# A kernel for one decoder step: 32 of 384 dense tokens take their first expert layer from fetched rows

## The chip, the cores and the metric

The kernel runs on one core of a Trainium2 chip. The metric is the device time of one execution in microseconds (us). The profile names the engines PE (TensorE, matrix products; PEld is its weight load), DVE (VectorE), ACT (ScalarE), POOL (GpSimd) and SP (SyncE, which here only issues DMAs). All data is float32; a product is formed from rounded "hi" parts and "lo" remainders in three matrix products.

## What is computed

One decoder layer on 512 prompt tokens and 32 sample tokens: attention, an output projection, and then the expert layer (PEER) that this text is about. The reference of the expert layer, cut:

```python
q = (xt @ w_query).reshape(PEER_BLOCK, PEER_HEADS, D_QUERY)      # 8 heads
s1 = einsum("thc,nc->thn", q[..., :half], k1)                    # 128 keys each
s2 = einsum("thc,nc->thn", q[..., half:], k2)
v1, i1 = top_k(s1, 16);  v2, i2 = top_k(s2, 16)
cand = v1[..., :, None] + v2[..., None, :]                       # 256 sums
top, pos = top_k(cand, 16)                                       # 16 of them
eidx = (i1 * 128 + i2) at pos                                    # 16 experts per head
g = softmax(top)
hid = einsum("thkd,td->thk", u_tab[eidx], xt)                    # first expert layer
a = g * gelu(hid)
out = einsum("thk,thkd->td", a, v_tab[eidx])                     # second expert layer
```

Each token has 8 heads of 16 chosen experts, 128 in all, out of 16384. A row of `u_tab` or `v_tab` is 1024 numbers, 4 KB.

## The kernel before, in words

The 544 tokens are tiles of 128 (the last has the 32 samples). Tokens 0 to 127 and the samples are **fetched**: their 160 sets of expert rows (each 128 rows of 4 KB, 512 KB) are gathered by indirect DMAs of POOL, and DVE forms a dot product with each (`multiply`, L1508; "dot" below). Tokens 128 to 511, 384 of them, are **dense**: for each of the 128 tiles of 128 experts PE multiplies all experts with all 384 tokens (`hidden_product`, L1426, 24 matmuls of 384 columns, output `hp`), ACT applies the gelu and a DMA stores the result; a gate matrix, built by small matmuls from one-hot rows, later says which values count.

A tile of `u_experts` (`uw`) has to be split first: ACT rounds it (`uhi`, L1420) and then POOL (L1424) or DVE (L2050) subtracts to get `ulo`. Tile m can't be split before PE is done with tile m - 2, and PE can't begin tile m before `ulo` is there. SP issues the load of tile m once tile m - 4 has been split.

After the attention the order on every engine is written out by hand, in stages:

- **Route.** `route_on_tensor` takes 8 heads in turn: two query products (48 matmuls of 272 columns), two sets of key scores, and 4 dense tiles per head (tiles 0 to 31). ACT copies the scores to `sc`, for which it needs DVE to have read the head before (`qs["read"]`). `route_on_vector` does the selection for a head in 18 linked steps (`LINKS`; each link waits for the one before), and then copies top values and indices (L1795 to L1797). POOL splits tiles and query weights.
- **QX.** 16 more dense tiles (32 to 47). When DVE has ended head 7 it prepares the tables: `first`, a subtraction, `eidx` (L1806), `sample_idx` (L1808), which count in `table_prep`; then SP spreads the sample indices over the partitions, and the softmax follows. Three transposes of `I1`, `I2` and `GG` come behind tiles 45, 46 and 47 on PE (`MIX` is 13); the first two need `table_prep` 2, the third 3.
- **Turns.** Six turns of 12 tiles (48 to 119), each with 16 groups of one-hots (DVE and ACT build them, PE multiplies them, ACT evacuates), 12 splits and 20 or 25 dots on DVE. Before the first turn DVE splits tile 49, builds two groups and does 5 dots (`FIRST_DOTS`).
- **GX.** Tiles 120 to 127 with the last 15 dots.
- **Values.** The second expert layer on PE, about 2,300 matmuls of 512 columns, until the end.

Dots go through nine buffers (`LOOK`): five of `gathered` and four of `vw`. POOL requests row set n + 9 when dot n is done.

## Time and profile before

| | us |
|---|---|
| median of 3 runs | 1698.84 (1697.75 to 1703.23) |
| the profiled execution | 1703.0 |
| its span, first to last instruction | 1701.4 |
| PE busy | 1622.1 (95%) |
| DVE busy | 1353.9 (80%) |
| ACT busy | 777.5 (46%) |
| POOL busy | 613.5 (36%) |
| three line groups of `hp` matmuls (1024 each) | 354.0, 344.8, 343.5 |

The three `hp` groups overlap one another, since matmuls are pipelined: their busy times can't be added, and what a matmul costs is the distance between two starts. The shares are means over stages with different limits, so the stages have to be read one by one.

### The profile page before, as it was taken

Reading aid. Unit: us, or ns where it says so; the run is one execution under the profiler, and the core shown is the slowest. Engines: PE = TensorE matmul, PEld = TensorE weight load, DVE = VectorE, ACT = ScalarE, POOL = GpSimd, SP = SyncE. Lnnn points to the kernel's source line nnn. Section 1 sums busy time; section 2 is a strip of 40 time slices with the busy share of each in tenths; the row PEclk is TensorE's granted clock in tenths of the full one; section 3 lists DMA queues with packets and bytes.
Section 4 is the critical chain, followed back from the end, with each engine's and each line's share of the span. In section 5 each row is a group of like instructions: output and inputs, shape, how many; then the busy total and the mean of one; then the engine's idle time right before and its main releaser. Section 6 shows DMA issues by size and latency. Waiting matters only on the chain.

```text
span 1701.4 us, 27754 instructions
## 1 busy us (share of the span) xinstructions
PE 1622.1 (95%) x9666; PEld 1460.0 (86%) x9666; DVE 1353.9 (80%) x3162; ACT 777.5 (46%) x1273; POOL 613.5 (36%) x538
## 2 busy tenths in 40 slices
PE   5999988798999999989999999999999999999997
PEld 4999744497999999989999999997888888888886
DVE  4324585353799999979999999987999999999996
ACT  4222373233434433367777767753333333333334
POOL 0000380054444444654334334432343333433320
PEclk9999997997999999999999999999999999999999
DMA  3342562722343333499999999999999999999991
GB/s 119 106 164 92 167 190 91 264 89 77 114 148 109 122 114 109 156 364 375 384 372 393 387 367 393 400 405 388 404 403 399 404 404 399 405 403 399 402 366 53
DMA packets 158621, 463.54 MB, mean 272 GB/s; under 512 B 18224, under 2 KB 64432, under 8 KB 154546
## 3 DMA queue, kind: packets, MB, share of 16 engines
q1 hardware_dynamic: 98930, 248.59, 39.7%
q0 software_dynamic: 50944, 178.96, 27.6%
q10 hardware_dynamic: 8640, 34.61, 5.1%
q8 instruction: 62, 1.02, 0.2%
q14 instruction: 45, 0.37, 0.1%
HBM read 406.12 MB, written 57.63 MB: 273 GB/s over the span
## 4 chain that ended last, share of the span: by engine, by line
PE 60%; DVE 13%; POOL 3%; DMA 2%; issue 1%; ACT 1%; another core or an unknown queue 0%; SPq 0%; ACTq 0%; POOLq 0%
PE va L230 10%; PE va L232 10%; PE va L231 10%; PE hp L230 6%; PE hp L231 6%; PE hp L232 6%; DVE gathered L1511 3%; DVE og L2039 3%; DVE ulo L2050 3%; PE ggp L1979 2%; DVE vw L1511 2%; PE qzp L230 2%; PE qzp L232 2%; PE qzp L231 2%; PE qsp L1680 1%
## 5 line engine op out<-in xcount | busy, mean ns | idle before, releaser
L230 PE MATMUL hp<-mid_hi,uhi 128*128 128x384 f32 x1024 | 354.0, 346 | 9.9 <-DVE ulo L2050 3.6
L231 PE MATMUL hp<-mid_lo,uhi 128*128 128x384 f32 x1024 | 344.8, 337 | 0.0
L232 PE MATMUL hp<-mid_hi,ulo 128*128 128x384 f32 x1024 | 343.5, 335 | 0.0
L230 PE MATMUL va<-vhi,ahi 128*128 128x512 f32 x768 | 299.8, 390 | 2.8 <-DVE hid L1511 2.1
L232 PE MATMUL va<-vhi,alo 128*128 128x512 f32 x768 | 299.5, 390 | 0.0
L231 PE MATMUL va<-vlo,ahi 128*128 128x512 f32 x768 | 299.3, 390 | 0.0
L1909 POOL DMA_INDIRECT gathered<-in_v_experts,eidx x160 | 175.6, 1098 | 310.3 <-DVE acc L2359 221.5
L230 PEld LDWEIGHTS hp<-mid_hi,uhi 128*128 128x128 f32 x1024 | 192.9, 188 | 15.0 <-DVE ulo L2050 5.8
L232 PEld LDWEIGHTS hp<-mid_hi,ulo 128*128 128x128 f32 x1024 | 193.0, 188 | 0.0
L231 PEld LDWEIGHTS hp<-mid_lo,uhi 128*128 128x128 f32 x1024 | 192.8, 188 | 0.0
L1420 ACT ACTIVATE uhi<-uw 128x1024 fp32r<-128x1024 f32 x126 | 132.8, 1054 | 116.1 <-PE hp L232 114.6
L1424 POOL TENSOR_TENSOR ulo<-uw,uhi 128x1024 fp32r<-128x1024 f32 x47 | 120.0, 2552 | 151.9 <-ACT uhi L1420 151.8
L230 PEld LDWEIGHTS va<-vhi,ahi 128*128 128x128 f32 x768 | 144.5, 188 | 34.3 <-DVE hid L1511 2.6
L232 PEld LDWEIGHTS va<-vhi,alo 128*128 128x128 f32 x768 | 144.5, 188 | 30.3
L231 PEld LDWEIGHTS va<-vlo,ahi 128*128 128x128 f32 x768 | 144.6, 188 | 30.0
L2359 DVE SCALAR_TENSOR_TENSOR acc<-gathered,coef,acc 128x1024 f32<-128x1024 f32 x128 | 164.2, 1283 | 4.2 <-DMA gathered<-in_v_experts,eidx 1.7
L1490 POOL DMA_INDIRECT gathered<-in_u_rows,eidx x96 | 104.7, 1090 | 165.2 <-DVE hid L1511 151.2
L1925 ACT ACTIVATE vhi<-vw 128x1024 fp32r<-128x1024 f32 x68 | 72.1, 1060 | 135.3 <-PE va L232 130.0
L2146 ACT ACTIVATE gst<-ggp 128x512 f32<-128x512 f32 x96 | 108.2, 1134 | 53.8 <-PE ggp L1979 40.1
L2039 DVE TENSOR_SCALAR og<-iota,chunkT 128x128 f32<-128x128 f32 x384 | 124.5, 367 | 0.0
L1925 ACT ACTIVATE vhi<-more_v 128x1024 fp32r<-128x1024 f32 x60 | 63.6, 1060 | 120.6 <-PE va L232 113.6
L1511 DVE CUSTOM_DVE_ANT_0 gathered<-gathered,x2p 128x1024 f32<-128x1024 f32 x96 | 113.5, 1212 | 5.0 <-DMA gathered<-in_u_rows,eidx 5.0
(328 smaller groups left out, 3448.6 us busy)
## 6 DMA issues: line engine op xcount, KB each, us to landing
uw<-in_u_experts SPq DMA_DIRECT2D x128, 512.0 KB
vw<-in_v_experts SPq DMA_DIRECT2D x68, 512.0 KB
more_v<-in_v_experts SPq DMA_DIRECT2D x60, 512.0 KB
gate_matrix<-gst ACTq DMA_DIRECT2D x12, 2048.0 KB
hidden_values<-gelu_out SPq DMA_DIRECT2D x72, 192.0 KB
hd_mid<-hidden_values SPq DMA_DIRECT2D x8, 1536.0 KB
gt_mid<-gate_matrix SPq DMA_DIRECT2D x8, 1536.0 KB
hd_freed<-hidden_values SPq DMA_DIRECT2D x7, 1536.0 KB
```

Of the source, the lines that this page charges most:

```text
L230: nc.tensor.matmul(out, a_hi, b_hi, start=first, stop=False)
L231: nc.tensor.matmul(out, a_hi, b_lo, start=False, stop=False)
L232: return nc.tensor.matmul(out, a_lo, b_hi, start=False, stop=last)
L1420: nc.scalar.activation(uhi[:, i], uw[:, r], ACT.Copy).then_inc(u_hi, 1)
L1424: nc.gpsimd.tensor_tensor(ulo[:, i], uw[:, r], uhi[:, i].bitcast(F32), ALU.subtract).then_inc(u_lo, 1)
L1490: nc.gpsimd.indirect_dma_start(buffers[to], None, u_table, bass.IndirectOffsetOnAxis(ap=eidx[:, row, b:b + 1], axis=0)).then_inc(gathered[ ...
L1511: nc.vector.tensor_tensor_reduce(out=buffers[to], in0=buffers[to], in1=x2p[:, b // SG], scale=1.0, scalar=0.0, op0=ALU.mult, op1=ALU.add, ...
L1909: nc.gpsimd.indirect_dma_start(gb[:, b], None, v_table, bass.IndirectOffsetOnAxis(ap=eidx[:, r, b:b + 1], axis=0)).then_inc(row_landed[b], 16)
L1925: nc.scalar.activation(vhi[:, m % GT], source, ACT.Copy).then_inc(xs["vhi"], 1)
L2039: last = nc.vector.tensor_scalar(og[:, i % RING, k], iota[:], col(0), col(2), ALU.is_equal, ALU.mult)
L2146: nc.scalar.activation(gst[:, u, :, 4 * r:4 * r + 4].rearrange("p i t -> p t i"), gp[i % 2][:], ACT.Copy).then_inc(gs["ev"], 1)
L2359: nc.vector.scalar_tensor_tensor(acc0[:], gb[:, c], coef[:, r, c:c + 1], acc0[:], ALU.mult, ALU.add).then_inc(xs["s0"], 1)
```

## The change

The last 32 of the 384 dense tokens (tokens 480 to 511, partitions 96 to 127 of token tile 3) take their first expert layer from fetched rows. Their 32 x 128 rows are 32 sets of 128 rows: 4 sets per head (`OWN_SLOTS`), each with 4 groups of 32 partitions. In parts:

1. Every `hp` product is 352 columns wide (`DENSE`) and not 384. The gelu is as wide; the last 32 columns of `gelu_out` are set to 1, once, by POOL.
2. Behind each head's selection DVE writes the 16 expert numbers of these tokens to `own_stage`, and SP spreads them with 4 small DMAs to `own_index` (`own_spread`).
3. POOL requests the 4 sets of head j - 2 in turn j, each behind a split (`own_fetch`); of heads 6 and 7 in QX.
4. DVE forms their 4 dots (`own_dot`) in head j behind links 10, 12, 14 and 16; the dots of heads 6 and 7 stand behind the tables. The tokens' own rows are read from PSUM (`x2own`).
5. ACT applies the gelu to them, SP brings them back with 4 DMAs (`own_act`), and DVE multiplies them into `GG` ahead of `table_prep` 3.
6. The splits of tiles 42 and 43 go from POOL to DVE (`LENT` is 10), behind the first own dots of head 6.
7. Of the 160 other dots 15 come before the turns (`FIRST_DOTS` 15, three of them ahead of `table_prep` 3, nine ahead of tile 49's split), 130 in the turns (`TURN_DOTS`) and 15 in GX; before it was 5, 140 and 15.
8. The loops over heads on SP, POOL, ACT, PE and DVE are written out.

```diff
-                last = mm3(hp[i][:, :TD], uhi[:, i, k], ulo[:, i, k], x2hi[:, k, P:SEQ], x2lo[:, k, P:SEQ],
+                last = mm3(hp[i][:, :DENSE], uhi[:, i, k], ulo[:, i, k], x2hi[:, k, P:P + DENSE], x2lo[:, k, P:P + DENSE],
                            k == 0, k == KD - 1)
...
-        FIRST_DOTS = ROW
-        TURN_ROWS = (ROW, ROW - 1)
+        LENT = 10
+        EARLY = (5, 7, 8, 9, 9, 9)
+        OWN_LINKS = (10, 12, 14, 16)
+        FIRST_DOTS, BEFORE_TABLE, BEFORE_TURNS = 15, 3, 9
+        TURN_DOTS = (22, 21, 22, 21, 22, 22)
...
+            elif n:
+                pool.wait_ge(own["dot"], (NH - (n < ROW)) * OWN_SLOTS)
             fetch(pool, n % LOOK, row, b)
...
+            def own_spread(sp, j):
+                sp.wait_ge(own["picked"], j + 1)
+                if j >= 2:
+                    sp.wait_ge(own["dot"], (j - 1) * OWN_SLOTS)
+                for g in range(OWN_GROUPS):
+                    sp.dma_start(own_index[g * OWN:(g + 1) * OWN, j % 2], own_stage[mine, g * OWN_SLOTS:(g + 1) * OWN_SLOTS]).then_inc(own["index"], 16)
+
+            def own_fetch(pool, j, n):
+                if n == 0:
+                    pool.wait_ge(own["index"], 16 * OWN_GROUPS * (j + 1))
...
+                nc.gpsimd.indirect_dma_start(own_buffers[j % 2][n], None, u_table,
+                                             bass.IndirectOffsetOnAxis(ap=own_index[:, j % 2, n:n + 1], axis=0)).then_inc(own_row[j % 2], 16)
+
+            def own_dot(dve, j, n):
+                dve.wait_ge(own_row[j % 2], 16 * OWN_SLOTS * (j // 2 + 1))
+                to = own_buffers[j % 2][n]
+                nc.vector.tensor_tensor_reduce(out=to, in0=to, in1=x2own[:], scale=1.0, scalar=0.0,
+                                               op0=ALU.mult, op1=ALU.add, accum_out=own_hid[:, j, n:n + 1]).then_inc(own["dot"], 1)
...
+                for e in range(2, LENT):
+                    u_split_lo(pool, RT * NH + e, e % 2, e % UR)
+                    if e < 2 + OWN_SLOTS:
+                        own_fetch(pool, NH - 2, e - 2)
+                for n in range(OWN_SLOTS):
+                    own_fetch(pool, NH - 1, n)
+                for n in range(EARLY[0]):
+                    request(pool, n)
+                pool.wait_ge(u_lo, RT * NH + LENT + 1 + 3)
+                for i, e in enumerate(range(LENT + 2, QX + 1)):
+                    u_split_lo(pool, RT * NH + e, e % 2, e % UR)
+                    for n in range(EARLY[i], EARLY[i + 1]):
+                        request(pool, n)
...
+                        if j >= 2 and links[0] in own_at:
+                            own_dot(dve, j - 2, own_at[links[0]])
                         dve.wait_ge(qs["chain"], j * LINKS + links[0])
...
+                dve.wait_ge(u_lo, RT * NH + LENT - 1 + 3)
+                for u in range(2):
+                    for n in range(u * OWN_SLOTS // 2, (u + 1) * OWN_SLOTS // 2):
+                        own_dot(dve, NH - 2, n)
+                    split_lo(dve, RT * NH + LENT + u, (LENT + u) % 2, (LENT + u) % UR)
+                for n in range(OWN_SLOTS):
+                    own_dot(dve, NH - 1, n)
```

What stands in a row on the engines, at the places that matter. **DVE, the second half of a head's selection**, before (L1775 and L1776 are link 10, L1788 link 13, L1792 links 15 to 17):

```order
468 L1775 TENSOR_SCALAR ab<-ab 128x80
469 L1776 TENSOR_SCALAR ab<-ab 128x80
470 L1732 REGISTER_ALU
471 L1777 CAST abf<-ab 128x240
472 L1732 REGISTER_ALU
473 L1778 SCALAR_TENSOR_TENSOR rank<-abf 128x5x16
474 L1780 SCALAR_TENSOR_TENSOR rank<-abf 128x5x16
475 L1732 REGISTER_ALU
476 L1784 TENSOR_TENSOR eq<-ranks,rank 128x2560
```

And now, in head 2:

```order
564 L1866 TENSOR_SCALAR ab<-ab 128x80
565 L1867 TENSOR_SCALAR ab<-ab 128x80
566 L1601 ISA gathered,own_hid<-gathered,x2own 128x1024
567 L1601 ISA own_hid 128x1
568 L1868 CAST abf<-ab 128x240
569 L1869 SCALAR_TENSOR_TENSOR rank<-abf 128x5x16
570 L1871 SCALAR_TENSOR_TENSOR rank<-abf 128x5x16
571 L1601 ISA gathered,own_hid<-gathered,x2own 128x1024
572 L1601 ISA own_hid 128x1
573 L1875 TENSOR_TENSOR eq<-ranks,rank 128x2560
```

A dot of 1024 columns stands behind link 10 and behind link 12; two more follow behind links 14 and 16. **DVE behind head 7**, from the sample index on, before:

```order
499 L1808 SCALAR_TENSOR_TENSOR sample_idx<-I 32x128
500 L1811 COPY eidx<-spread_idx 128x32
501 L1813 TENSOR_REDUCE sm<-GG 128x40
502 L1815 RECIPROCAL sm<-sm 128x40
503 L1817 TENSOR_TENSOR GG<-GG,sm 128x640
504 L1819 COPY sgate<-GG 128x32x4
505 L2050 TENSOR_TENSOR ulo<-uw,uhi 128x1024
```

And now, with the splits of tiles 42 and 43 at L1533:

```order
900 L1904 SCALAR_TENSOR_TENSOR sample_idx<-I 32x128
901 L1601 ISA gathered,own_hid<-gathered,x2own 128x1024
902 L1601 ISA own_hid 128x1
903 L1601 ISA gathered,own_hid<-gathered,x2own 128x1024
904 L1601 ISA own_hid 128x1
905 L1533 TENSOR_TENSOR ulo<-uw,uhi 128x1024
906 L1601 ISA gathered,own_hid<-gathered,x2own 128x1024
907 L1601 ISA own_hid 128x1
908 L1601 ISA gathered,own_hid<-gathered,x2own 128x1024
909 L1601 ISA own_hid 128x1
910 L1533 TENSOR_TENSOR ulo<-uw,uhi 128x1024
```

Two dots now stand ahead of tile 42's split, and two more ahead of tile 43's. **POOL in QX**, before (the 18 splits run from head 7's tiles to tile 47):

```order
210 L1424 TENSOR_TENSOR ulo<-uw,uhi 128x1024 x18
211 L1490 DMA gathered<-in_u_rows,eidx 128x1024 x4
212 L1424 TENSOR_TENSOR ulo<-uw,uhi 128x1024
213 L1997 COPY chunkT<-slotT 128x96
```

And now, from the splits of tiles 38 to 41 on:

```order
270 L1429 TENSOR_TENSOR ulo<-uw,uhi 128x1024 x4
271 L1595 DMA vw<-in_u_rows,own_index 128x1024 x4
272 L1499 DMA gathered<-in_u_rows,eidx 128x1024 x5
273 L1429 TENSOR_TENSOR ulo<-uw,uhi 128x1024
274 L1499 DMA vw<-in_u_rows,eidx 128x1024 x2
275 L1429 TENSOR_TENSOR ulo<-uw,uhi 128x1024
276 L1499 DMA vw<-in_u_rows,eidx 128x1024
277 L1429 TENSOR_TENSOR ulo<-uw,uhi 128x1024
278 L1499 DMA vw<-in_u_rows,eidx 128x1024
279 L1429 TENSOR_TENSOR ulo<-uw,uhi 128x1024 x2
280 L2106 COPY chunkT<-slotT 128x96
```

Nine requests now stand ahead of the split of tile 44 (row 273), and four more between the splits of tiles 44 and 47.

## Rows read from the trace of the kernel before

**Rows 1.** Busy time by stage: start:end, length, engines with counts, PE clock, DMA share, GB/s

```profile
432.00:718.00 286.00, 283.57 (x1840) 278.16 (x1839) 261.30 (x1103) 109.76 (x155) 140.92 (x56) 1.00 0.39 129
718.00:744.00 26.00, 24.01 (x144) 22.84 (x142) 16.05 (x36) 14.75 (x22) 19.31 (x16) 1.00 0.75 279
744.00:1127.00 383.00, 378.15 (x2431) 376.48 (x2432) 373.68 (x910) 276.96 (x471) 152.32 (x148) 1.00 1.00 386
1127.00:1180.00 53.00, 48.18 (x251) 44.42 (x251) 39.21 (x61) 19.08 (x27) 18.72 (x17) 0.98 1.03 390
1180.00:1701.00 521.00, 512.50 (x2253) 422.46 (x2252) 470.56 (x562) 201.79 (x271) 170.58 (x155) 0.99 0.95 371
```

**Rows 2.** Waits from 432 to 722 us: who waited for whom, total, times, longest

```profile
DVE V L1740 <- ACT sc L1627: 28.7, 1, 28.7
...
ACT sc L1626 <- DVEq L1746: 20.2, 4, 10.0
```

**Rows 3.** Order of time, DVE: start, length, engine, line, operation [idle before]

```profile
432.20 2.04 DVE L1740 MAX8 V<-sc 128x8 f32<-128x128 f32 x10 [28.65 <-ACT sc L1627]
...
680.35 2.03 DVE L1740 MAX8 V<-sc 128x8 f32<-128x128 f32 x10 [0.38 <-issue]
...
718.35 0.20 DVE L1801 COPY first<-GG 128x40 f32<-128x40 f32 x1
...
721.74 0.27 DVE L1808 SCALAR_TENSOR_TENSOR sample_idx<-I 32x128 uint32<-32x128 f32 x1
...
735.40 0.28 DVE L2038 TENSOR_SCALAR oh<-iota,chunkT 128x128 f32<-128x128 f32 x1
...
738.29 1.21 DVE L1511 CUSTOM_DVE_ANT_0 gathered<-gathered,x2p 128x1024 f32<-128x1024 f32 x1
...
744.00 0.34 DVE L2038 TENSOR_SCALAR oh<-iota,chunkT 128x128 f32<-128x128 f32 x1
```

**Rows 4.** Order of time, PE: matmuls of 384 and 512 columns

```profile
690.16 0.33 PE L230 MATMUL hp<-mid_hi,uhi 128*128 128x384 f32 x1
690.33 0.34 PE L231 MATMUL hp<-mid_lo,uhi 128*128 128x384 f32 x1
...
1400.34 0.39 PE L232 MATMUL va<-vhi,alo 128*128 128x512 f32 x1
1400.56 0.39 PE L230 MATMUL va<-vhi,ahi 128*128 128x512 f32 x1
```

**Rows 5.** Order of time, DVE: dots that follow one another

```profile
739.43 1.21 DVE L1511 CUSTOM_DVE_ANT_0 gathered<-gathered,x2p 128x1024 f32<-128x1024 f32 x1
...
740.57 1.21 DVE L1511 CUSTOM_DVE_ANT_0 gathered<-gathered,x2p 128x1024 f32<-128x1024 f32 x1
```

**Rows 6.** A DVE group from 432 to 720 us: busy, mean ns, idle before

```profile
L1788 DVE TENSOR_TENSOR eq<-eq,XF 128x1280 bf16<-128x1280 bf16 x16 | 31.1, 1982 | 1.2
```

**Rows 7.** The same line by instruction: duration in ns, min/median/max

```profile
L1788 DVE TENSOR_TENSOR eq<-eq,XF x16: 944/1936/3161, 458.4 to 709.9; 128x1280 bf16<-128x1280 bf16 x16
```

**Rows 8.** Order of time, POOL: a split and a request

```profile
723.16 2.41 POOL L1424 TENSOR_TENSOR ulo<-uw,uhi 128x1024 fp32r<-128x1024 f32 x1 [1.49 <-ACT uhi L1420]
...
727.13 0.95 POOL L1490 DMA_INDIRECT gathered<-in_u_rows,eidx  x1 [0.30 <-issue]
```

**Rows 9.** Order of time, ACT: the copy ahead of a tile's split

```profile
661.97 1.06 ACT L1420 ACTIVATE uhi<-uw 128x1024 fp32r<-128x1024 f32 x1 [2.72 <-PE hp L232]
```

**Rows 10.** Order of time, DVE: the wait for four small DMAs that SP issued

```profile
725.84 0.20 DVE L1811 COPY eidx<-spread_idx 128x32 uint32<-128x32 uint32 x1 [3.82 <-DMA spread_idx<-sample_idx]
```

**Rows 11.** PE alone, behind its pause before the route: busy, granted clock, DMA

```profile
400.00:417.00 17.00, 14.93 (x88) 0.80 0.45 148
```

**Rows 12.** DVE waits from 744 to 1127 us

```profile
DVE ulo L2050 <- ACT uhi L1420: 7.3, 7, 2.3
```

**Rows 13.** The chain of work: start, length; key scores of heads 2 and 3

```profile
480.85 1.23 PE qsp L1680 x10
...
512.49 1.23 PE qsp L1680 x10
```

More of the change, by code:

```diff
@@ L58 @@
 NG = NK // GT
+OWN = 32
+DENSE = TD - OWN
+OWN_GROUPS = P // OWN
+OWN_SLOTS = TOPK // OWN_GROUPS
+OWN_TILE = TT - 2
 NSLOT = NH * TOPK
@@ L1512, in multiply, with dot, split_lo @@
                                            op0=ALU.mult, op1=ALU.add, accum_out=out).then_inc(gs["dot"], 1)
+        def dot(dve, n):
+            row, b = divmod(n, ROW)
+            if n == SG:
+                dve.wait_ge(gs["x2p"], 2)
+            dve.wait_ge(gathered[n % LOOK], 16 * (n // LOOK + 1))
+            multiply(dve, n % LOOK, b, hid[:, row, b:b + 1])
+        def split_lo(dve, m, i, r):
+            dve.wait_ge(u_hi, m + 1)
+            nc.vector.tensor_tensor(ulo[:, i], uw[:, r], uhi[:, i].bitcast(F32), ALU.subtract).then_inc(u_lo, 1)
+        own = {n: sem("own_" + n) for n in ("x2", "copied", "ones", "picked", "index", "dot", "act", "back")}
+        own_row = [sem(f"own_row{i}") for i in range(2)]
+        own_buffers = [[gb[:, b] for b in range(1, ROW)], [vw[:, i] for i in range(GT)]]
+        mine = slice(P - OWN, P)
         with ExitStack() as st:
@@ L1555, in route_on_sync @@
                 sp.dma_start(slot_sum[:], A["slot_sum"]).then_inc(x2r_spread, 16)
-                with sp.Fori(0, NH - 1) as j:
+                for j in range(NH - 1):
                     for u in range(2):
@@ L1608, in route_on_scalar @@
                 act.wait_ge(qs["clr"], 1)
+                act.wait_ge(own["ones"], 1)
                 def split(n, u, j):
@@ L1634, in route_on_scalar @@
                 act.sem_inc(qs["hi"], 2)
-                with act.Fori(0, NH - 1) as j:
-                    turn(j, False)
-                turn(NH - 1, True)
+                for j in range(NH):
+                    turn(j, j == NH - 1)
+                    if j == 0:
+                        act.wait_ge(own["x2"], 16 * OWN_GROUPS)
+                        act.wait_ge(fs["split_lo"], 2 * TT)
+                        nc.scalar.activation(x2own[:], gb[:, 0], ACT.Copy).then_inc(own["copied"], 1)
                 for e in range(QX):
@@ L1698, in route_on_tensor @@
                     hidden_product(pe, i, i % 2)
-                with pe.Fori(1, NH) as j:
+                for j in range(1, NH):
                     for u in range(2):
@@ L1724, in route_on_vector @@
                 ut = [(u, t) for u in range(2) for t in range(TT)]
-                with dve.Fori(0, NH) as j:
+                own_at = {link: n for n, link in enumerate(OWN_LINKS)}
+                for j in range(NH):
                     links = [0]
@@ L2000, in turn @@
                 j = 2 * pair + half
-                first = FIRST_DOTS + (pair * PAIR_ROWS + half * ROW) * ROW
-                n = (ROW if last else TURN_ROWS[half]) * ROW
+                first, n = FIRST_DOTS + sum(TURN_DOTS[:j]), TURN_DOTS[j]
                 at = 0
@@ L2014, in gate_on_gpsimd @@
             cut(0, 0, True)
-            for n in range(SG, LOOK):
+            for n in range(EARLY[-1], LOOK):
                 request(pool, n)
@@ L2040, in build_one_hots @@
                 last.then_inc(gs["oh"], 1)
-            def dot(n):
-                row, b = divmod(n, ROW)
-                dve.wait_ge(gathered[n % LOOK], 16 * (n // LOOK + 1))
-                multiply(dve, n % LOOK, b, hid[:, row, b:b + 1])
-            def split_lo(m, i, r):
-                dve.wait_ge(u_hi, m + 1)
-                nc.vector.tensor_tensor(ulo[:, i], uw[:, r], uhi[:, i].bitcast(F32), ALU.subtract).then_inc(u_lo, 1)
             def turn(pair, half, last):
                 j = 2 * pair + half
-                first = FIRST_DOTS + (pair * PAIR_ROWS + half * ROW) * ROW
-                rows_here = ROW if last else TURN_ROWS[half]
+                first, here = FIRST_DOTS + sum(TURN_DOTS[:j]), TURN_DOTS[j]
                 at, built = 0, AHEAD
@@ L2156, in gate_on_scalar @@
             over_turns(act, turn)
+            for where in ("seam", "narrow"):
+                nc.scalar.activation(gates[where][0][:, :, DENSE:], ge[:, 0, DENSE:].unsqueeze(1).broadcast_to([P, GT, OWN]), ACT.Copy)
             for e in range(GX):
```

119 lines of the change are left out of this document (78 added, 41 removed).

## The prediction

> **What bounds the kernel now.** I read the busy times by stage first [rows 1]. PE is busy 95% of the span, but it is not the only full engine. From 432 to 718 us, the route, PE is busy 283.6 of 286 us and DVE 261.3. From 744 to 1127, the turns, PE has 378.2 of 383 and DVE 373.7, and the DMA engines are full as well (1.00, 386 GB/s). From 1180 on PE is full by itself. So each edit has to be asked which of the two engines it loads.
>
> For the route the waits decide it [rows 2]. DVE waits for scores once, 28.7 us before head 0, and never again. ACT, which copies the scores, waits four times, 20.2 us in all and once 10.0 us, until DVE has read the head before. The 24.7 us that DVE seems to be idle in the route are small gaps between its links: 1.2 us ahead of the eight L1788 pairs, 0.15 us a link [rows 6]; 18 links in 8 heads make 21.6 of it. DVE starts head 0 at 432.20 and ends head 7 at 718.35 [rows 3]: 286.2 us for 8 heads, 35.8 us each, back to back. PE runs its dense tiles in what that leaves. **The route is DVE's**, and PE's 99% there is work that it does ahead, until in QX it comes to the transposes that need DVE's tables. In the turns both are within 3% of their limit: DVE has 9.3 us of idle time, 7.3 of them for ACT's copies, and these wait for PE [rows 12].
>
> **What the narrower products give PE.** Matmuls of 384 and 512 columns start 0.17 and 0.22 to 0.23 us after one another [rows 4]. 128 columns more cost some 53 ns, 0.41 ns a column, and 32 columns fewer are 13.3 ns, or 0.32 us for the 24 matmuls of a tile, and 41 us for 128 tiles: 10 in the route, 5 in QX, 23 in the turns, 2.6 in GX. The gelu copies get shorter too, which no one waits for.
>
> **What it costs, and where.** I walk along DVE's time, and cost everything against the profiled execution.
>
> Term 1, the route. In heads 2 to 7 DVE does 24 own dots. A dot starts 1.14 us before the next instruction [rows 5]: 27.4 us. Each stands in a gap of 0.15 us that was idle [rows 6], which gives back 3.6. The 8 index computations are as small as the copy at 718.35, 0.2 us or less [rows 3]: 1.3. Sum 25, and nothing hides it, since DVE waits for no one there. Its gathers should be there in time: POOL requests them one head ahead (turn j of POOL runs while DVE is in head j - 1). The 16.8 MB of own rows meet DMA engines at 0.39 of their time [rows 1]. PE's 10 us of the route are worth nothing; it waits longer for DVE's read. Head 7 ends at 743.4.
>
> What I can't read off is how DVE and POOL hold one another up. The L1788 multiply takes 0.94 us at best and 3.16 at worst [rows 7], and the long ones lie on POOL's splits of 2.4 us [rows 8]. Against its best this line alone loses 31.1 - 16 x 0.94 = 16 us in the route [rows 6]; by the other short operations of the same part it is some 40 to 50 in all, an estimate from that row. POOL has as many splits as before, so I take the loss as unchanged, with 15 us less and 12 more as bounds: less if POOL, which now stands at an index wait, is still during a head's second half; more if all heads meet it as the worst ones do. The Trainium skill (SBUF — State Buffer, section "SBUF: two separate sides") says that a DVE instruction in a two-port mode or with two SBUF inputs and a GpSimd instruction exclude each other for their whole length. The spread of L1788 agrees with it. By that rule the own dots, with one operand in PSUM, aren't held up by POOL; were they, up to 2.2 us on each of 24 would be lost, and the time would be near 1786 us.
>
> Term 2, from the end of head 7 to the first turn. Before, this took 718.35 to 744.0 us [rows 1, 3], 25.7 us, and PE went on with its tiles meanwhile. Now PE stands in front of tile 42, since DVE itself has to split it. Counted from the end of head 7: tables 3.6 us (718.35 to 722.0) [rows 3], two own dots 2.3, the split 1.2; PE starts tile 42 at 7.1. Tiles 42 and 43 take 24 x 0.16 = 3.85 us each: 15. Tile 44 is POOL's. POOL has its 4 own requests of head 7 behind the index (3.8 us for four small DMAs) [rows 10], 1.25 us each [rows 8]; then requests 1 to 4, which must wait for DVE's 28th own dot at 9.4, until 14.5; and the split, 2.4: PE starts tile 44 at 17. For tiles 45 to 47 POOL has 1 or 2 requests and a split in each round against a copy on ACT of 1.06 us [rows 9] behind the tile two before: 22, 26.5 and, with the transposes, 31 us. Tile 47 is done at 35. Then as before: ACT's copy and DVE's split of tile 49, to 38; the first one-hots 2.9 (735.40 to 738.29) [rows 3], 41; and six dots, 48. DVE's eight last own dots, the softmax and nine other dots lie beside PE's tiles here and cost nothing as long as the tiles take 28 us. I add 3 us for the clock. In front of the route PE paused, and behind that ran at a mean clock of 0.80 [rows 11], that is partly at 1.2 GHz rather than 2.4; here it will pause for about 10 us before tile 42, and somewhat more before tile 35, where POOL waits for head 6's index. The bound is nothing to 7 us. Sum 51 against 25.7: +25.
>
> Term 3, the turns. DVE has ten dots fewer there: 373.7 - 11.4 = 362.3. PE would need 378.2 - 23 = 355. So DVE is the bound, and its idle time, which was for PE's sake, should fall from 9.3 to some 6: 368 for 383 us, -15. Bounds: -11 if the idle time stays, -21 if it goes. The bytes fall with the dots (5.2 MB of 148), so the DMA rate stays at 387 GB/s, which it has now.
>
> Term 4, GX and the values: the last dots end as late as their fetches, -1 of PE's 2.6. The values are unchanged. The two copies of ones are short.
>
> Sum: +25 +25 -15 -1 = +34, so 1703.0 becomes 1737. The profiled execution lay 4.2 us above the median of the runs, so I expect **1733 us**, with 1715 to 1752 from the bounds.
>
> **The rivals.** A: all heads meet POOL as the last two do. Head 7 took 38.0 us (680.35 to 718.35) [rows 3] when PE was held at DVE's pace, against 35.8 on average. With six heads at 38.0 + 4.2, head 7 ends 37 us later, not 25: 1746 us. For it: PE will be held in every head. Against it: the phase shifts with the dots. B: POOL is in the way. It waits for the index of head j - 2 ahead of splits that PE needs; if that makes scores late by 3 us in each of six heads, DVE starves for 18 us: 1751. Against it: DVE must have ended head j - 2 well before ACT may copy the scores of head j anyway. C: the matmuls don't get shorter with 352 columns, because something else than the columns sets the distance between starts. Then only terms 2 and 3 lose a little: 1738. Against it: 384 and 512 columns differ by what 128 columns take at 0.41 ns each [rows 4]. D: the clash between POOL and DVE largely goes, 25 us of it: 1708, still slower. E, the other side: DVE is not the bound of the route. It decides from the point where a head with its dots takes DVE less than PE: 31.6 us a head (480.85 to 512.49) [rows 13], less 4 x 0.32, is 30.4. Then PE's 41 us count in full, 1658, or with tile 42's wait for DVE still there, some 1680. Against it: DVE's one wait in 290 us [rows 2] and 35.8 us a head without any dot.
>
> The Trainium skill (TensorE: Matmul & The Clock Gate, section "What's actually happening") has PE fall to half its clock after an idle stretch. The row behind the pause [rows 11] shows that here; by the page alone the pauses would cost a few us each, the same as my bound.
>
> **How the numbers follow.** Forecast 0.55, A 0.22, B 0.07, C 0.05, D 0.07, E 0.04. The predicted time is the forecast's. The range for 8 in 10 takes in A and C and the edge of D: 1714 to 1753. A measurement of this kernel can tell 0.3%, 5 us, from no change. Slower by more than that is all but E and a part of D: 0.93; within it 0.03; faster 0.04.
>
> **What the changed profile would show.** The starts of `hp` matmuls 0.160 us apart. Heads 2 to 7 of 39 to 41 us on DVE, heads 0 and 1 as before, end of head 7 near 743. PE with a pause of some 10 us before tile 42, and about as much before tile 35, and half clock beside it. The first turn's one-hots near 794, tile 120 on PE near 1162, the values as long as they were. Wrong would be: DVE waiting for scores or for `own_row` in the route, which brings rivals B or a late gather; heads shorter than 37 us, which brings D; a turn stage above 375 us.

## The result and the profile after

The changed kernel takes 1746.81 us (median of 4 runs, 1741.07 to 1749.77). The kernel before, run beside it, took 1699.9 (median of 4): 1.027 times the time, with 1.0237 to 1.0303 as the 95% interval. That is slower, 47 us, and inside the predicted range of 1714 to 1753; the forecast was 14 us too low. A sum that is right in its total can be wrong in its terms, and three of these four terms were off by 6 to 13 us, one of them the other way.

The busy times by stage, of the changed kernel (columns as in [rows 1]; the stages are the route, the end of head 7 to the first turn, the turns, and, behind GX, the values):

```profile
431.00:736.00 305.00, 270.46 (x1764) 262.15 (x1762) 285.87 (x1160) 87.41 (x135) 156.44 (x80) 0.93 0.46 157
736.00:800.00 64.00, 38.52 (x217) 37.59 (x217) 41.62 (x75) 24.33 (x38) 38.86 (x32) 0.83 0.82 293
800.00:1174.00 374.00, 363.25 (x2434) 355.84 (x2435) 363.98 (x890) 270.65 (x463) 144.08 (x139) 0.99 1.00 382
...
1226.00:1748.00 522.00, 513.26 (x2255) 423.07 (x2253) 470.34 (x562) 201.82 (x271) 175.44 (x155) 0.99 0.95 370
```

Against [rows 1]: the route is 305 us for 286, the stretch behind it 64 for 26, the turns 374 for 383, the rest as it was. With the edges read to the instruction:

| | before | after | change | forecast |
|---|---|---|---|---|
| route, start of head 0 to end of head 7 | 286.1 | 305.2 | +19.1 | +25 |
| end of head 7 to first turn | 25.6 | 63.4 | +37.8 | +25 |
| turns, to tile 120 on PE | 383.1 | 374.0 | -9.1 | -15 |
| GX and values | 574.3 | 574.5 | +0.2 | -1 |
| span (head 0 began 1.2 earlier) | 1701.4 | 1748.2 | +46.8 | +34 |

**Matmuls.** The `hp` products do start 0.16 us after one another, where they started 0.17 apart in [rows 4] (order of time, PE):

```profile
677.76 0.32 PE L235 MATMUL hp<-mid_hi,uhi 128*128 128x352 f32 x1
677.92 0.32 PE L236 MATMUL hp<-mid_lo,uhi 128*128 128x352 f32 x1
```

**Waits from 432 to 800 us** (who waited for whom, total, times, longest), where [rows 2] had 20.2 us of ACT's wait for DVE:

```profile
ACT sc L1706 <- DVEq L1837: 56.4, 5, 13.8
...
POOL gathered L1595 <- DMA own_index<-own_stage: 28.8, 3, 13.8
...
PE hp L235 <- POOL ulo L1429: 26.4, 3, 13.0
```

ACT, and so PE, now wait 56.4 us for DVE to have read the head before: PE is held at DVE's pace, as the prediction's first part has it. DVE is in no row of the route: it never waits for scores or own rows there. POOL waits for the own indices, and PE for POOL's splits, three times. Each of PE's long waits is followed by a start at half clock. Its four restarts from tile 35 on, in order of time, and the busy times and granted clock right behind the third:

```profile
703.76 0.66 PE L235 MATMUL hp<-mid_hi,uhi 128*128 128x352 f32 x1 [13.02 <-POOL ulo L1429]
...
741.16 0.66 PE L235 MATMUL hp<-mid_hi,uhi 128*128 128x352 f32 x1 [6.08 <-DVE ulo L1533]
...
764.11 0.66 PE L235 MATMUL hp<-mid_hi,uhi 128*128 128x352 f32 x1 [12.34 <-POOL ulo L1429]
...
802.77 0.66 PE L235 MATMUL hp<-mid_hi,uhi 128*128 128x352 f32 x1 [9.36 <-DVE ulo L1533]
```

```profile
764.00:768.00 4.00, 3.89 (x14) 3.89 (x15) 4.00 (x6) 0.00 (x0) 3.51 (x4) 0.56 0.77 235
```

A matmul of 0.32 us takes 0.66 there, at a mean clock of 0.56, that is mostly at 1.2 GHz of its 2.4. The fourth restart is tile 50's, in the first turn: PE stands 9.36 us until DVE is done with its dots and splits that tile. The mean clock of 0.93 in the route has stretches at 1.2 GHz in it as well, at PE's shorter waits there (one of 6.26 us up to 555.78, and a clock of 0.50 from 552.5 to 559.2); PE has time to spare in the route.

**The end of head 7 to the first turn**, the part that was mis-sized. First POOL in order of time:

```profile
740.08 1.86 POOL L1595 DMA_INDIRECT vw<-in_u_rows,own_index  x1 [9.94 <-DVE own_hid L1601]
...
745.65 0.94 POOL L1595 DMA_INDIRECT vw<-in_u_rows,own_index  x1 [0.30 <-issue]
...
750.61 0.94 POOL L1499 DMA_INDIRECT gathered<-in_u_rows,eidx  x1 [0.30 <-issue]
760.76 0.93 POOL L1499 DMA_INDIRECT gathered<-in_u_rows,eidx  x1 [9.21 <-DVE eidx L1914]
761.71 2.35 POOL L1429 TENSOR_TENSOR ulo<-uw,uhi 128x1024 fp32r<-128x1024 f32 x1
...
785.45 1.00 POOL L1499 DMA_INDIRECT gathered<-in_u_rows,eidx  x1 [0.30 <-issue]
```

and DVE in the same stretch:

```profile
736.25 0.19 DVE L1897 COPY first<-GG 128x40 f32<-128x40 f32 x1
...
755.16 1.22 DVE L1601 CUSTOM_DVE_ANT_0 vw<-vw,x2own 128x1024 f32<-128x1024 f32 x1 [10.64 <-DMA vw<-in_u_rows,own_index]
...
759.74 0.19 DVE L1914 COPY eidx<-spread_idx 128x32 uint32<-128x32 uint32 x1
...
784.41 1.23 DVE L1533 TENSOR_TENSOR ulo<-uw,uhi 128x1024 fp32r<-128x1024 f32 x1 [2.94 <-ACT uhi L1425]
...
793.22 1.22 DVE L1520 CUSTOM_DVE_ANT_0 gathered<-gathered,x2p 128x1024 f32<-128x1024 f32 x1 [3.32 <-DMA gathered<-in_u_rows,eidx]
...
799.65 0.52 DVE L2146 TENSOR_SCALAR oh<-iota,chunkT 128x128 f32<-128x128 f32 x1
```

Read together (the first row names a dot as what ended POOL's wait; by the program it waits there for the index of head 7): POOL has its four own requests out at 746.6 and requests 0 to 3 at 751.5. The fifth of the other requests, the first whose index comes from the samples, waits 9.21 us for DVE's `eidx` copy (L1914). That copy stands behind the four own dots of head 7, and they wait 10.64 us, until 755.16, for rows requested from 740.08 to 746.6; all four have to be there, and the last was requested at 745.65, 9.5 us before. Tile 44's split stands behind that request on POOL (761.71), and PE behind the split (764.1). A gather, a table and a split that have nothing to do with one another stand in a row.

### The profile page after: what moved, and what is told of

Read it like the earlier page. It is cut to its first block, busy times and chain, and to the rows that moved or that the text cites. A ratio compares the mean times of both kernels' runs of the same rounds, so it can differ in the third digit from the quotient of the medians.

```text
span 1748.2 us, 27385 instructions
## 1 busy us (share of the span) xinstructions
PE 1604.6 (92%) x9666; PEld 1433.8 (82%) x9666; DVE 1392.1 (80%) x3237; ACT 756.4 (43%) x1264; POOL 643.8 (37%) x569
## 4 chain that ended last, share of the span: by engine, by line
PE 35%; DVE 30%; DMA 8%; issue 4%; POOL 2%; ACT 2%; SPq 0%; DVEq 0%; ACTq 0%; POOLq 0%
PE va L235 10%; PE va L237 10%; PE va L236 10%; DMA hidden_values<-gelu_out 5%; DVE og L2147 3%; DVE gathered L1520 3%; DVE ulo L1533 3%; DVE vw L1520 2%; DVE X L1842 1%; DVE X L1834 1%; DVE eq L1879 1%; DVE sc L1835 1%; DVE oh L2146 1%; DVE eq L1883 1%; DVE eq L1875 1%
## 5 line engine op out<-in xcount | busy, mean ns | idle before, releaser
L235 PE MATMUL hp<-mid_hi,uhi 128*128 128x352 f32 x1024 | 348.3, 340 | 53.1 <-POOL ulo L1429 26.4
L236 PE MATMUL hp<-mid_lo,uhi 128*128 128x352 f32 x1024 | 335.8, 328 | 0.0
L237 PE MATMUL hp<-mid_hi,ulo 128*128 128x352 f32 x1024 | 334.7, 327 | 0.0
L2018 POOL DMA_INDIRECT gathered<-in_v_experts,eidx x160 | 180.5, 1128 | 306.4 <-DVE acc L2459 210.8
L235 PEld LDWEIGHTS hp<-mid_hi,uhi 128*128 128x128 f32 x1024 | 197.6, 193 | 65.5 <-DVE ulo L1533 35.3
L236 PEld LDWEIGHTS hp<-mid_lo,uhi 128*128 128x128 f32 x1024 | 197.7, 193 | 0.0
L237 PEld LDWEIGHTS hp<-mid_hi,ulo 128*128 128x128 f32 x1024 | 197.0, 192 | 0.0
L235 PEld LDWEIGHTS va<-vhi,ahi 128*128 128x128 f32 x768 | 144.6, 188 | 35.9 <-DVE hid L1520 3.5
L1499 POOL DMA_INDIRECT gathered<-in_u_rows,eidx x96 | 101.1, 1053 | 181.3 <-DVE hid L1520 158.4
L1429 POOL TENSOR_TENSOR ulo<-uw,uhi 128x1024 fp32r<-128x1024 f32 x45 | 110.8, 2462 | 103.3 <-ACT uhi L1425 103.2
```

The costliest lines, as they stand in the source:

```text
L235: nc.tensor.matmul(out, a_hi, b_hi, start=first, stop=False)
L236: nc.tensor.matmul(out, a_hi, b_lo, start=False, stop=False)
L237: return nc.tensor.matmul(out, a_lo, b_hi, start=False, stop=last)
L1429: nc.gpsimd.tensor_tensor(ulo[:, i], uw[:, r], uhi[:, i].bitcast(F32), ALU.subtract).then_inc(u_lo, 1)
L1499: nc.gpsimd.indirect_dma_start(buffers[to], None, u_table, bass.IndirectOffsetOnAxis(ap=eidx[:, row, b:b + 1], axis=0)).then_inc(gathered[ ...
L2018: nc.gpsimd.indirect_dma_start(gb[:, b], None, v_table, bass.IndirectOffsetOnAxis(ap=eidx[:, r, b:b + 1], axis=0)).then_inc(row_landed[b], 16)
```

## The experiments

Runs were made together with the kernel before; each ratio is against that. Stage lengths are of the profiled execution. In runs that change the dots' width I give two stages by name: **route** (286.1 before, 305.2 after) and **turns 2 to 6**, from tile 60 to tile 120 on PE, which leaves out the first turn, whose start depends on how far PE is ahead (323.4 before, 316.3 after). How well such lengths repeat: the route, the same work in both, took 286.1 us in the kernel before and in its run with thin dots, and turns 2 to 6 took 316.0 to 317.3 in four forms of the changed kernel that differ only ahead of them.

### Own dots of 16 columns

```diff
-nc.vector.tensor_tensor_reduce(out=to, in0=to, in1=x2own[:], ...
+nc.vector.tensor_tensor_reduce(out=to[:, :16], in0=to[:, :16], in1=x2own[:, :16], ...
```

> The changed kernel, but each of the 32 own dots covers 16 columns and not 1024 (so the first layer of those 32 tokens is left incomplete); fetches, waits and order stay. Theory (VectorE is the bound from the route on, and the 24 own dots of the route lengthen it by their own length): a dot falls from 1.14 to about 0.1 us, so head 7 ends some 23 to 25 us earlier than 736, near 712; the way from there to the first turn gets some 6 us shorter; total near 1716 us, 30 below the changed kernel. Rival (what counts is the added fetches, index waits on GpSimd and the PE that they hold back): head 7 still ends near 730 and the total stays above 1735.

Measured 1722.17 us, ratio 1.0116 (1.0096 to 1.0137). Route 284.8, end of head 7 to first turn 58.6. Order of time, DVE, a thin dot and what follows it:

```profile
667.41 0.16 DVE L1601 CUSTOM_DVE_ANT_0 gathered<-gathered,x2own 128x16 f32<-128x16 f32 x1
...
667.63 0.28 DVE L1868 CAST abf<-ab 128x240 f32<-128x240 uint32 x1
```

A thin dot still takes 0.22 us of DVE's path (667.41 to 667.63), a whole one 1.14 [rows 5], so 24 x 0.92 = 22.1 us should go; 20.4 did. **The dots are the route's loss**, and a route with all the requests, spreads and waits but thin dots is as long as that of before (284.8, 286.1), though by two differences that cancel: heads 0 and 1 are 5.3 us longer, heads 2 to 7 together 6.7 shorter. The rest of the slowdown, 1722 against 1702.5 for the kernel before beside it, is the stretch behind head 7, which got only 4.8 us shorter.

### The products 384 wide again

```diff
-last = mm3(hp[i][:, :DENSE], ..., x2hi[:, k, P:P + DENSE], ...
+last = mm3(hp[i][:, :TD], ..., x2hi[:, k, P:SEQ], ...
```

> The changed kernel with the first-layer products 384 columns wide again, everything else the same. Theory (PE waits for VectorE in the route, so only the turns feel it): the route ends as late as now, 736; six tiles before the turns cost 2 us; the turns, where PE would have 363 + 23 = 386 us of work against 374 now, grow by 8 to 12; total +10 to +15, 1757 to 1762 us. Rival (PE's columns count everywhere): +41, 1788 us.

Measured 1756.12 us, ratio 1.031 (1.029 to 1.0331). The route is 303.3, the stretch behind it 64.4, the turns 382.2 for 374.0: all that the narrower products bring lies in the turns, 8.2 us of the 41 that PE saves. The total lies just under the 1757 to 1762 of the theory and far under the rival's 1788.

### The kernel before, with 352 wide products and nothing else

```diff
-last = mm3(hp[i][:, :TD], ..., x2hi[:, k, P:SEQ], ...
+last = mm3(hp[i][:, :TD - 32], ..., x2hi[:, k, P:SEQ - 32], ...
```

> The kernel before with products 352 wide and nothing in exchange: the first layer of the last 32 dense tokens is left out and their values are 1. It tells what the narrower product is worth by itself, at most. Theory (VectorE bounds route and turns): the route ends at 718 as before, the turns lose only the time in which VectorE waits for PE, 5 to 8 of 383 us, the rest 1 to 3; total 1689 to 1694 us. Rival (PE bounds the turns and they shrink by its 23 us): 1674 or less; if PE bounds all, 1659.

Measured 1700.67 us (median of 10), ratio 0.9994 (0.9979 to 1.001). **The narrowing by itself is worth nothing**, where I had expected 1689 to 1694. The turns gained 4.7 us and the route lost 5.9 (292.0), where heads 0 and 1 took 37.9 and 38.4 for 35.1 and 35.9. No DVE instruction of the route was changed; that POOL's splits fall on other DVE instructions when the tiles are faster fits the last experiment below, but no run shows it by itself.

### What bounds the turns: four runs

The kernel before, with its 160 dots 16 columns wide, then that with 352 wide products, then that with fetches of 64 bytes a row as well, and the changed kernel with thin dots:

```diff
-nc.vector.tensor_tensor_reduce(out=buffers[to], in0=buffers[to], in1=x2p[:, b // SG], ...
+nc.vector.tensor_tensor_reduce(out=buffers[to][:, :16], in0=buffers[to][:, :16], in1=x2p[:, b // SG, :16], ...
...
-nc.gpsimd.indirect_dma_start(buffers[to], None, u_table,
+nc.gpsimd.indirect_dma_start(buffers[to][:, :16], None, A["u_rows"].rearrange("n (a d) -> (n a) d", d=16),
```

> The kernel before with each of its 160 first-layer dots over 16 columns and not 1024 (their first layer is left incomplete). It takes 140 x 1.05 = 147 us of work from VectorE in the turns. Theory (in the turns PE, at 378 of 383 us, is right behind VectorE): the turns fall only to 375 to 380, total -5 to -12. Rival (VectorE is far the slower one there): the turns fall by 20 us or more.

> The run before this one with products 352 wide as well (32 tokens' first layer left out besides). Against it it tells what the narrower product is worth once VectorE isn't full in the turns. Theory: PE's 23 us of the turns show now, turns near 355, total 20 to 26 us under the run before it; the route, VectorE's, still gives nothing. Rival (the DMA engines, at 1.00 and 386 GB/s, are the next bound): 10 us or less.

> The kernel before with products 352 wide, dots of 16 columns, and each of the 160 first-layer fetches of 64 bytes a row and not 4 KB (that layer is left incomplete for the fetched tokens, and left out for 32 others). It takes about 70 of 144 MB from the DMA engines in the turns. Against the run with full fetches (turns 368.7 us at 400 GB/s, PE 355 us of work): theory (the DMA engines are the third limit of the turns, close behind PE and VectorE): turns fall to 356 to 360 us, DMA share far below 1. Rival (the rest is how PE, ACT and the splits wait for one another): turns stay at 366 or more.

> Changed kernel in which the 160 other dots multiply 16 columns and not 1024 (the fetches are whole, the own dots are whole); what they leave out makes the first expert layer of the fetched tokens wrong. It takes some 130 us of VectorE's work out of the turns. Theory: in the changed kernel VectorE bounds the turns (busy 364 of 374 us), while in the kernel before TensorE did, so that the same edit, which moved nothing there (385 for 383 us), here shortens the turns to what TensorE (355) and the transfers (142.6 MB at the 400 GB/s of the run with narrower products and thin dots: 356.5) allow: 358 to 364 us. The stretch from the end of head 7 to the first turn loses the six dots that follow the split of tile 49, some 7 us, to 56 to 58. Together 1724 to 1731 us beside 1747. Rival: the pace of the turns is set by the chain of groups and splits, whichever engine is full, or by the transfers at 382 GB/s; then the turns stay at 371 to 376 us and only the 7 us are gained: 1738 to 1742.

Measured: 1700.19 us (0.998, 0.9966 to 0.9995); 1692.62 (0.993, 0.9902 to 0.9958); 1677.17 (0.984, 0.9817 to 0.9864); 1730.86 (1.016, 1.0143 to 1.0178). Turns 2 to 6 of eight kernels, busy times, each row of its own trace. Before, before with thin dots, changed with 384 wide products:

```profile
803.70:1127.10 323.40, 321.98 (x2084) 320.85 (x2082) 316.34 (x771) 235.84 (x401) 126.64 (x124) 1.00 1.00 386
```

```profile
807.10:1128.20 321.10, 321.10 (x2083) 321.10 (x2082) 199.43 (x761) 235.99 (x401) 112.83 (x123) 1.00 0.99 388
```

```profile
857.40:1180.20 322.80, 322.27 (x2082) 321.00 (x2082) 309.08 (x756) 233.94 (x401) 114.36 (x116) 1.00 0.98 375
```

Before with 352 wide products, the changed kernel:

```profile
802.00:1123.30 321.30, 309.78 (x2084) 302.03 (x2082) 316.44 (x771) 233.71 (x401) 131.82 (x124) 1.00 1.00 389
```

```profile
857.30:1173.60 316.30, 308.86 (x2083) 302.02 (x2082) 308.80 (x757) 233.36 (x401) 121.22 (x116) 1.00 1.00 383
```

352 wide with thin dots, and with thin fetches as well:

```profile
808.70:1117.10 308.40, 303.10 (x2082) 301.86 (x2081) 197.89 (x764) 232.04 (x399) 117.02 (x124) 1.00 1.02 403
```

```profile
807.60:1108.90 301.30, 301.30 (x2083) 301.30 (x2081) 195.21 (x764) 235.02 (x401) 117.38 (x123) 1.00 0.65 218
```

The changed kernel with thin dots:

```profile
852.10:1156.20 304.10, 302.73 (x2083) 301.73 (x2082) 196.67 (x750) 232.90 (x401) 107.70 (x116) 1.00 1.01 398
```

The first block is PE's limit: with 384 columns these five turns take 321 to 323 us, whether DVE has 316 us of work or 199. The second is DVE's: with PE busy for 309 or 310 they take DVE's work (316, 309) and 5 to 7.5 us. With neither, the DMA engines are the third, 308.4 us at 403 GB/s, and only without them PE's own need at 352 columns shows, 301.3: it fell by 19.8 us from 321.1, where 60 tiles at the forecast 0.32 make 19.2. In the changed kernel taking DVE's dots away gives 12.2 us (316.3 to 304.1), where in the kernel before it gave 2.3. **So before the change PE and DVE bounded these turns together, each to within some 2 us; after it DVE alone does**, with the DMA engines 12 us behind. As expectations three of the four missed. In the first run's whole turns stage the time even rose by 2 us (385.1 for 383.1, expected 375 to 380): its first turn took 64.1 for 59.7. The stage began 2.6 us earlier against PE's tile 49, since the five dots before it were thin; for the other 2 us I have no cause. The second run's turns took 368.7 and not 355, as its rival had it. The third run's took 365.2, between its theory (356 to 360) and its rival (366): turns 2 to 6 gained 7.1 us over the second run, but the first turn lost 3.6 (63.9 for 60.3). Its total gained more, since the stretch ahead of the turns and GX with the values are shorter too (17.1 for 24.5, and 565.9 for 574.7). The last run's turns took 360.5 (358 to 364 expected). It gained 1.2 us before the turns and not 7: the dots there wait for their rows, however thin.

### The tables ahead of head 7's own dots

```diff
-                for n in range(OWN_SLOTS):
-                    own_dot(dve, NH - 1, n)
                 dve.wait_ge(table_spread, ...)
                 nc.vector.tensor_copy(eidx[:, :, SG:], ...)
+                for n in range(OWN_SLOTS):
+                    own_dot(dve, NH - 1, n)
```

> The changed kernel, but VectorE copies the spread sample indices ahead of the four own dots of head 7, not behind them, so that GpSimd's fifth request, and behind it the split of tile 44, need not wait for these rows to land. Theory (that wait put PE to rest for 12.7 us from 751.5 to 764.2): tile 44 starts near 754 and the total falls by 6 to 10 us, to 1737 to 1741. Rival (the landing of head 7's rows at 755 sets the end anyway, by way of the gelu, the way back and the gate table): 0 to -3 us.

Measured 1744.46 us, ratio 1.0234 (1.0216 to 1.0251). PE starts tile 44 9 us earlier after the end of head 7 (19.0 for 27.9 us), and the first turn only 1.9 (61.5 for 63.4). POOL in order of time:

```profile
751.92 2.35 POOL L1429 TENSOR_TENSOR ulo<-uw,uhi 128x1024 fp32r<-128x1024 f32 x1
759.62 0.95 POOL L1499 DMA_INDIRECT vw<-in_u_rows,eidx  x1 [5.34 <-DVE own_hid L1601]
...
761.84 2.37 POOL L1429 TENSOR_TENSOR ulo<-uw,uhi 128x1024 fp32r<-128x1024 f32 x1
```

The fifth request waits no more, but the sixth goes into a buffer that head 7's own dots have to leave, and tile 45's split stands behind it. One wait gives way to the next, and the stretch that the theory was about gained 1.9 us and not 6 to 10. In total it is 2.4 us by the medians and some 6 by the ratios, since the kernel before was 2.6 slower beside this run.

### Fewer splits on POOL and the tables first

```diff
-        LENT = 10
-        EARLY = (5, 7, 8, 9, 9, 9)
+        LENT = 14
+        EARLY = (5, 9)
+        FETCH, SPREAD = 8, 8
```

with the edit above; tiles 42 and 43 go back to POOL, DVE splits 46 and 47, and head 6's requests come six tiles later.

> The late request of the run before, the copy of the spread indices ahead of head 7's dots, and VectorE splits tiles 46 and 47 in place of 42 and 43, so that PE can do tiles 42 to 45 while VectorE is still in head 7. Theory (the way from head 7 to the turns is long because six tiles and three waits for landing rows stand in a row): the route ends at 736 as before, the first turn starts near 776 to 782 and not at 800, total 1722 to 1730. Rival (the landing of head 7's rows and the way back of their gelu set the start of the turns whatever stands beside them): less than 8 us, 1740.

Measured 1737.23 us, ratio 1.0197 (1.0168 to 1.0227), the fastest form of the changed kernel that leaves no work out, and still 2% slower than before. The theory had 1722 to 1730, its rival 1740. The stretch behind head 7 is 49.1 for 63.4 us, the route 309.3 for 305.2. The waits from 715 to 790 us name what is next in line:

```profile
PE ggp L1803 <- DVE GG L1927: 14.2, 1, 14.2
...
DVE vw L1602 <- DMA vw<-in_u_rows,own_index: 7.5, 1, 7.5
```

PE has done its tiles up to the last transposes, and waits 14.2 us for the gates of the own tokens, which need the dots of head 7, which need rows requested after head 7's index.

### Own rows of 64 bytes

```diff
-nc.gpsimd.indirect_dma_start(own_buffers[j % 2][n], None, u_table,
+nc.gpsimd.indirect_dma_start(own_buffers[j % 2][n][:, :16], None, A["u_rows"].rearrange("n (a d) -> (n a) d", d=16),
```

with thin own dots.

> The changed kernel with own dots of 16 columns and own fetches of 64 bytes a row (the first layer of the 32 tokens is left incomplete). Against the run with thin dots but full fetches (route end 713.7, from there to the first turn 58.6 us, total 1722): theory (head 7's own rows land 9 us after their request, and softmax, the fifth request and the way back queue behind them): 58.6 falls to 46 to 50 us, route unchanged, total 1711 to 1714. Rival (the order of six tiles is enough by itself): 56 or more, total 1720.

Measured 1720.5 us, ratio 1.0087 (1.006 to 1.0113), against 1722.17 (1.0116) with thin dots alone; 1711 to 1714 were expected, and the total is the rival's. Tile 44 starts 19.5 us behind the end of head 7 (23.4 with thin dots alone, 27.9 in the changed kernel, 17 in the forecast), the first turn 55.3 (58.6). DVE still waits for a row of 64 bytes (waits from 715 to 770 us):

```profile
DVE vw L1601 <- DMA vw<-in_u_rows,own_index: 6.7, 1, 6.7
DVE GG L1926 <- DMA own_act<-own_hid: 5.6, 1, 5.6
```

It was 10.6 with whole rows, with thin dots too. So the size of the transfer is 4 us of the wait. Of the other 6.7, which begin at 723.0, the last of the four requests takes until 723.8, and 5.9 pass from there until DVE goes on at 729.7. I had expected the larger part from the size. And the 3.3 us that this stretch gained were lost again in the turns (376.1 for 372.8), for which I have no cause.

### Head 6's own requests later

```diff
-                    if e < 2 + OWN_SLOTS:
-                        own_fetch(pool, NH - 2, e - 2)
+                    if FETCH <= e < FETCH + OWN_SLOTS:        # FETCH = 6, was 2
+                        own_fetch(pool, NH - 2, e - FETCH)
```

> The changed kernel, but GpSimd requests the own rows of head 6 behind the splits of tiles 38 to 41 and not 34 to 37, and SyncE spreads their index three tile loads later. In the changed kernel GpSimd stood 13.8 us for that index, and PE rested 13.5 us in front of tile 35. Theory (PE is ahead of VectorE in the route, so that rest is free and only moves to tile 42): total within 3 us of the changed kernel, 1743 to 1750. Rival (PE's rest is lost time): -10 to -13 us, 1735.

Measured 1750.96 us, ratio 1.0275 (1.0247 to 1.0303), no difference from the changed kernel. PE's waits for POOL's splits there fall from 13.0 to 7.3 us, its wait in front of tile 42 grows from 6.1 to 14.6, and nothing is won, as the theory had it. But head 6 takes 45.7 us on DVE, and head 7 33.6, for 37.5 and 39.8. DVE in order of time:

```profile
651.47 1.22 DVE L1602 CUSTOM_DVE_ANT_0 vw<-vw,x2own 128x1024 f32<-128x1024 f32 x1
...
676.50 2.41 DVE L1868 TENSOR_SCALAR ab<-ab 128x80 uint32<-128x80 uint32 x1
...
685.75 5.98 DVE L1880 TENSOR_TENSOR eq<-eq,XF 128x1280 bf16<-128x1280 bf16 x2
```

and POOL beside it:

```profile
651.20 2.62 POOL L1429 TENSOR_TENSOR ulo<-uw,uhi 128x1024 fp32r<-128x1024 f32 x1 [6.40 <-ACT uhi L1425]
...
676.46 2.39 POOL L1429 TENSOR_TENSOR ulo<-uw,uhi 128x1024 fp32r<-128x1024 f32 x1 [0.34 <-ACT uhi L1425]
...
684.28 3.57 POOL L1429 TENSOR_TENSOR ulo<-uw,uhi 128x1024 fp32r<-128x1024 f32 x1 [1.39 <-ACT uhi L1425]
688.29 2.63 POOL L1429 TENSOR_TENSOR ulo<-uw,uhi 128x1024 fp32r<-128x1024 f32 x1 [0.43 <-ACT uhi L1425]
```

An instruction of 0.20 us takes 2.41, as long as the split it meets, and POOL's split takes 3.57 rather than 2.4 where DVE was first. The two multiplies of the last DVE row, 0.95 us each at best, take 5.98 beside two splits. The dot at 651.47, one operand of which is in PSUM, lies wholly beside a split and takes its 1.22. Where the splits fall in a head is worth 8 us of that head.

## Why the prediction came out as it did

The time is inside the range, and with +46.8 for +34 the direction and most of the size are right. Some of that is luck: terms 2 and 3 were 19 us short together, and term 1 was 6 too large. The measured time is also within 1 us of rival A's 1746, whose mechanism did not happen.

**The first part, the route is DVE's: right.** ACT's wait for DVE's reading, behind which PE stands, grew from 20.2 to 56.4 us, DVE never waited, and 41 us of PE's work taken away alone changed nothing (1700.67).

**Term 1, +25: the dots right, the rest not, 6 us too large.** The working said 27.4 for 24 dots, less 3.6 of gaps, plus 1.3. DVE's busy time in the route rose by 285.87 - 261.3 = 24.6, which is the dots' 27.4 and the index computations' 1.5 (L1888, 8 x 188 ns), less some 4.3. These 4.3 are a remainder and were not measured by a run. The idle time fell by 24.7 - 19.1 = 5.6. The term that I took as unchanged, the clash with POOL, is the likely place. The line of [rows 6, 7], by group and by instruction, in the changed kernel:

```profile
L1879 DVE TENSOR_TENSOR eq<-eq,XF 128x1280 bf16<-128x1280 bf16 x16 | 21.0, 1351 | 1.2
```

```profile
L1879 DVE TENSOR_TENSOR eq<-eq,XF x16: 948/957/3147, 456.5 to 727.8; 128x1280 bf16<-128x1280 bf16 x16
```

Its median is now its best, 957 ns for 1936, and it lost 10 us of its 31.1. Other lines took most of that up:

```profile
L1844 DVE CAST XF<-X 128x160 bf16<-128x160 uint32 x8 | 7.5, 940 | 1.2
...
L1868 DVE CAST abf<-ab 128x240 f32<-128x240 uint32 x8 | 6.0, 754 | 0.3
```

They were 3.2 and 2.3 us before. The clash was bound at 15 less and 12 more, and if the remainder is the clash, 4 less it became. The net hides two larger changes, and the sign "heads 0 and 1 as before" failed. Head 2 begins, in the kernel before, the kernel before with 352 wide products, and the changed kernel (order of time, DVE):

```profile
503.17 2.04 DVE L1740 MAX8 V<-sc 128x8 f32<-128x128 f32 x10 [0.38 <-issue]
```

```profile
506.86 2.03 DVE L1742 MAX8 V<-sc 128x8 f32<-128x128 f32 x10 [0.40 <-issue]
```

```profile
507.28 2.02 DVE L1831 MAX8 V<-sc 128x8 f32<-128x128 f32 x10
```

Head 0 began at 432.20, 430.52 and 431.02. So heads 0 and 1, which have no own dot, took 71.0, 76.3 and 76.3 us: narrowing the products is enough to add the 5.3. Heads 2 to 7, with all 24 dots, grew only by 13.8 us (215.2 to 229.0), where 24 were in the sum. The Trainium skill's rule (SBUF — State Buffer, section "SBUF: two separate sides"), that such instructions of the two engines exclude each other for their whole length, agrees with the rows of the last experiment, and so does what it let me leave out: the own dots were not held up (1.23 us on average for 1.21). Rival A (every head like the last two), B and D did not happen, nor C: heads 2 to 7 took 37.3 to 39.8 us, where 39 to 41 were expected, and the products do start 0.16 us apart.

**Term 2, +25: direction right, 13 us too small, the largest error.** By its own steps, from the end of head 7: tile 42 at 4.9 us (forecast 7.1), tile 44 at 27.9 (17), first turn at 63.4 (51). The step that failed is "then requests 1 to 4 ... and the split, 2.4: PE starts tile 44 at 17". The requests are counted from 0. Requests 0 to 3 were out at 751.5, 15.3 us behind head 7, but request 4, which I had out at 14.5, only at 25.4 (761.7). I had let it wait for a dot alone and left out that it takes its index from the samples' table; and I had set the landing of head 7's own rows, on which that table depends by the order on DVE, at next to nothing. The 32 own gathers took from 4.3 to 9.8 us, the last one of head 7 9.5 (DMA to landing, by line):

```profile
L1595 POOL DMA_INDIRECT vw<-in_u_rows,own_index x16: 936/946/1865, 511.6 to 745.6; - x16
...
DMA to landing us min/median/max: 4.3/5.9/9.8
```

With the table's copy put first tile 44 starts at 19.0, and with thin own rows and dots at 19.5, both within 2.5 us of the forecast: the order of the copy and the length of the rows and dots ahead of it together cost the 11 us, and to take either away is nearly enough for this tile (though not for those behind it). From tile 44 on I had 31 us to the first turn. Tile 48 came 17.9 us behind tile 44 (forecast 18), tile 49's split and the one-hots were done at 24.6 (24), and then the six dots took 11.0 us and not 6.8: they waited for rows, 3.32 us for the second of them, requested at 785.45, 7.8 us before. That is the other 4.5. The 3 us for the clock were about right in size and partly wrong in place. Tiles 42 and 43 took from 741.2 to 751.5, 10.3 us for two times 3.85, but PE then waits for tile 44 anyway, so these 2.6 us cost nothing. Tile 44 took 5.5 us (764.11 to 769.60), 1.6 more than at full clock, and these count. Together 10.9 and 4.5 more, less the 3 that the steps already contain, are the 12.4 us from 51 to 63.4. The Trainium skill (TensorE: Matmul & The Clock Gate, section "What's actually happening") has the clock halved after an idle stretch, and the four restarts agree.

**Term 3, -15: the size off by 6, its reason half wrong.** DVE is the bound, as forecast. DVE's busy time in the turns came out at 364.0, where 362.3 was forecast. But "its idle time, which was for PE's sake, should fall from 9.3 to some 6" failed: it is 10.0, and the wait in [rows 12] is longer, not shorter (DVE waits from 800 to 1174 us):

```profile
DVE ulo L1533 <- ACT uhi L1425: 9.9, 13, 1.5
```

So -9 fell outside even the bound "-11 if the idle time stays". In the kernel before with narrow products it does fall, from 7.3 to 4.7 us. What keeps ACT's copies late in the changed kernel isn't settled; the gelu's own wait for its stored results is longer too, 37.7 us for 27.7. And the prediction saw both engines within 3% of their limit and then went on with DVE alone; the runs put them level before the change, 321 us for PE and 321 for DVE in the five turns.

**Term 4 and the values: right**, +0.2 for -1.

**What would have been the gain?** Of PE's 41 us, 8.2 were had, all of them in the turns, where 23 were to be saved. The 10 of the route and the 5 of QX went into waiting: with 384 wide products the route and the stretch behind it are no longer than with 352 (367.7 and 368.6 us together). The change adds work to DVE in the route, where DVE is the bound, to relieve PE, which is ahead there. Against 8 us stand 20 of dots in the route and 38 of a stretch in which PE is idle for 25 us, where it was idle for 2.

## What to carry over

Work taken off one engine is worth only what the stage's second limit leaves, and when three limits lie within 5% (PE 321, DVE 321, DMA engines 308 of 323 us) the stage hardly moves for any one of them (here 2 us): thin out one load at a time to find their order before you trade one for another. When requests, tables and splits are put in one in-order queue, list for the last thing in it everything that each one ahead waits for, by its own conditions, and give each gather its loaded landing time and not its idle one.
